# A state-space mixer on one NeuronCore: the gate of each group is projected two groups ahead instead of one

## What is computed

```
z, xbc, dt = split(h @ w_in)
xs, bm, cm = split(silu(dwconv(xbc)))
...
cb = einsum('bign,bjgn->bijg', ci, bi)
y = einsum('bijg,bijgr,bjgrp->bigrp', cb, decay, xdt)
y = y + einsum('bign,bigr,bgrpn->bigrp', ci, exp(cum), s)
...
y = (y_f + y_b[:, ::-1] + xs * d_gr)
return rms_norm_2(y * silu(z), norm_g) @ w_out
```

## Time and profile before

| | |
|---|---|
| Three runs | 2572.54, 2579.03, 2581.88 us; median 2579.03 us |
| The profiled execution | 2571.71 us, span 2570.1 us |
| PE busy | 2150.8 us, 84% of the span |
| DVE, ACT, POOL busy | 43%, 25%, 3% |
| Mean granted PE clock | 0.922 of full speed |
| The eight groups | from about 2152 us to 2296 us of the span |

### The profile page before, as it was taken

How to read it: one execution, slowest core, us unless ns; L and a number is a source line. 1 busy time by engine, 2 the same in 40 slices (tenths; PEclk the granted TensorE clock), 3 DMA queues, 4 the chain that set the end, 5 groups by cost and what they waited for, 6 DMA issues and landing times.

```text
span 2570.1 us, 31035 instructions
## 1 busy us (share of the span) xinstructions
PE 2150.8 (84%) x11646; PEld 1413.8 (55%) x11646; DVE 1110.2 (43%) x2058; ACT 644.6 (25%) x1212; POOL 68.8 (3%) x112
## 2 busy tenths in 40 slices
PE   6978688888968657885999878999977997997997
PEld 3457332334456422322445536888866886773996
DVE  0054321111153411112506535666673776863766
ACT  1134110111234100101302103111105544641332
POOL 1000100001000100001000000000010000000000
PEclk9979899999989788998999988999987997998999
DMA  6438779983448577985111021222211224323453
GB/s 190 140 111 276 255 305 401 406 328 122 140 148 284 177 295 310 406 329 196 66 66 66 33 82 66 99 99 99 99 55 59 100 73 154 118 92 138 174 187 115
DMA packets 153835, 440.42 MB, mean 171 GB/s; under 512 B 12176, under 2 KB 14656, under 8 KB 145360
## 3 DMA queue, kind: packets, MB, share of 16 engines
q1 hardware_dynamic: 145216, 414.88, 43.8%
q0 software_dynamic: 8464, 23.48, 3.0%
HBM read 534.63 MB, written 1.21 MB: 208 GB/s over the span
## 4 chain that ended last, share of the span: by engine, by line
PE 43%; ACT 4%; DVE 4%; DVEq 1%; issue 1%; DMA 1%; POOL 0%; ACTq 0%; SPq 0%; POOLq 0%
PE bank L1840 32%; PE bank L1914 10%; ACT UT L2208 1%; PE bank L1845 1%; DVE ARENA L2753 1%; ACT ARENA L2371 1%; DVE BN L2439 0%; ACT UH L2208 0%; DMA NEGM<-in_neg 0%; DVEq L2453 0%; DVE XA L2447 0%; ACT ARENA L2364 0%; ACT XHI L2208 0%; ACT ARENA L2184 0%; DMA ARENA<-cum_rows 0%
## 5 line engine op out<-in xcount | busy, mean ns | idle before, releaser
L604 PE MATMUL bank<-WA,XG 128*32 128x512 f32 x1536 | 187.5, 632 | 75.2 <-DMA WA<-in_expert_w_up 63.6
L1840 PE MATMUL bank<-W,UT 128*128 128x512 f32 (+2 forms) x704 | 238.2, 502 | 13.1 <-ACT XHI L2208 8.7
L464 PE MATMUL bank<-WD,XT 128*128 128x512 f32 (+1 forms) x576 | 239.9, 579 | 4.8 <-ACT XT L783 2.8
L2219 ACT ACTIVATE WPH<-W 128x1024 fp32r<-128x1024 f32 x128 | 135.4, 1070 | 371.3 <-PE bank L1840 198.2
L1840 PEld LDWEIGHTS bank<-W,UT 128*128 128x128 f32 x704 | 135.6, 204 | 114.2 <-issue 107.9
L1840 PE MATMUL bank<-UH,WPH 128*128 128x512 f32 (+1 forms) x512 | 174.0, 340 | 18.7 <-DVE WPL L2464 18.7
L464 PEld LDWEIGHTS bank<-WD,XT 128*128 128x128 f32 x576 | 109.7, 191 | 133.6 <-issue 128.4
L1840 PE MATMUL bank<-UL,WPH 128*128 128x512 f32 (+1 forms) x512 | 173.7, 339 | 0.0
L1840 PE MATMUL bank<-UH,WPL 128*128 128x512 f32 (+1 forms) x512 | 173.7, 339 | 0.0
L2464 DVE TENSOR_TENSOR WPL<-W,WPH 128x1024 fp32r<-128x1024 f32 x128 | 153.4, 1220 | 16.9 <-ACT WPH L2219 16.9
L604 PEld LDWEIGHTS bank<-WA,XG 128*32 128x32 f32 x1536 | 47.9, 115 | 204.0 <-issue 124.1
(11 more groups left out here) (370 smaller groups left out, 3345.7 us busy)
## 6 DMA issues: line engine op xcount, KB each, us to landing
WA<-in_expert_w_gate SPq DMA_DIRECT2D x32, 2048.0 KB
WA<-in_expert_w_up SPq DMA_DIRECT2D x32, 2048.0 KB
WC<-in_expert_w_down SPq DMA_DIRECT2D x32, 2048.0 KB
W<-in_ffn_w SPq DMA_DIRECT2D x64, 1024.0 KB, 6.6
WD<-in_ada_w SPq DMA_DIRECT2D x48, 1024.0 KB, 6.4
WA<-in_expert_w_gate SPq DMA_DIRECT2D x64, 512.0 KB
WA<-in_expert_w_up SPq DMA_DIRECT2D x64, 512.0 KB
WC<-in_expert_w_down SPq DMA_DIRECT2D x32, 1024.0 KB
```

Source lines behind the costliest of these rows:

```text
L464: last = nc.tensor.matmul(bank[r.bank(key)][:, 0:n], lhs[k], rhs[k], start=(k == 0), stop=(k == len(lhs) - 1))
L604: last = nc.tensor.matmul(bank[r.bank(key)][32 * g:32 * g + 32, :], xg[:, 4 * part + k, col:col + 32], WA[part][:, g, :, k, :], start=(par ...
L1840: return nc.tensor.matmul(bank[r.bank(key)][0:rows, cols[0]:cols[1]], lhs, rhs, start=start, stop=stop)
L2219: nc.scalar.activation(piece_view(WPH, q), piece_src(i, q), ACT.Copy).then_inc(hi_done, 1)
```

## The change

On PE `group_gate(1)` is issued behind `group_gate(0)`, ahead of the first group's outputs, and in turn g of the loop the gate of group g + 2 is projected instead of that of group g + 1. On ACT `gate(0)` is ahead of `segments(0)`, and `gate(g + 2)` stands in turn g where `gate(g + 1)` stood. Nothing else is changed: the banks, the two halves of Z and the lists of DVE, POOL and SP are the same.

```
             group_gate(0)
+            group_gate(1)
             for g in range(SG_):
                 group_outputs(g)
                 if g + 1 < SG_:
                     group_pre(g + 1)
-                    group_gate(g + 1)
+                if g + 2 < SG_:
+                    group_gate(g + 2)
                 if g >= 1:
                     group_turns(g - 1)
...
             act.wait_ge(x_whole, 1)
+            gate(0)
             segments(0)
             state_copy(0)
-            gate(0)
+            gate(1)
             act.wait_ge(ng_in, 16)
             for g in range(SG_):
                 if g + 1 < SG_:
                     segments(g + 1)
                     state_copy(g + 1)
-                    gate(g + 1)
+                if g + 2 < SG_:
+                    gate(g + 2)
                 if g >= 1:
                     turned_out(g - 1)
```

## The result

The changed kernel takes 2608.73 us (median of 4 runs, 2606.6 to 2615.26), the kernel before 2575.78 us (4 runs, 2572.49 to 2581.88). The ratio is 1.0129, with a 95% interval of 1.0099 to 1.0159: about 33 us slower. The profiled execution took 2615.26 us, span 2613.7 us.

A forecast was written before the change was run, and what follows sets the result against it. PE was taken to bound the loop before; the change's serial ACT-DVE chain adds 33.6 us up to T(7) and the end 3.9, so 37.5 us slower, 2616 from the median 2579.03; forecast 2615 us, range 2601 to 2624.

The forecast's parts named there:

- The start: Group 0: silu ahead of the exponentials, these 4.8 us late; PE's hole shrinks from 8.11 to about 5.1 us, clock low.
- T(0): End of group 0's 16 exponentials on ACT, put at 2173.36, 4.8 us late.
- The loop: Groups 2 to 7: waiting for `y_rdy` ahead of the exponentials makes a serial ACT-DVE chain, 21.8 us a turn against 16.4.
- six terms: Parts of a loop turn: 0.03, 1.37, 10.62 (DVE to `y_rdy`), 0.49, 0.85 and 8.42 us (load and exponentials), sum 21.8.
- the one term of 2.62 us: DVE's diagonals in each loop turn, counted within the 10.62 us of weights, diagonals and finish up to `y_rdy`.
- PE in time for the chain: In the loop PE's 15.66 us of work a turn fits the 21.8 us chain and costs it nothing, despite bank 2 waits.
- The end: Last outputs: PE idles some 9.6 us without a gate in turn 6, clock falls, `out_part` starts 3.9 us later relatively.
- T(7): End of group 7's 16 exponentials on ACT, put at 2317.8, 33.6 us later than before.
- The sum: Whole kernel: 33.6 + 3.9 = 37.5 us slower; 28.7 with the full clock throughout.
- The table load: ACT's function switches: 1.29 us from load to silu, no added drain; the skill page's 1.38 us would add about 8 us.
- The rival of the cold loop: PE runs the whole loop at the low clock, 31.3 us a turn, about 2663 us; chance 0.05.
- The rival of a gain: Hole at the start filled, `y_rdy` wait free, clock kept: up to 7.7 us faster, 2571 us; chance 0.02.

The follow-up runs named there:

- e1: The changed kernel with a third part of Z, so that gate(g) waits for the output of group g - 3; 2581.09 us, ratio to before 1.0031.
- e5: The changed kernel with DVE's finish of group g - 1 ahead of the diagonals of group g + 1; 2593.77 us, ratio to before 1.0084.
- e7: The changed kernel with the first half of each gate from group 2 on projected twice on PE; 2610.89 us in one execution.
- e2: The changed kernel with ACT's silus in the loop one group ahead as before, PE's order kept; 2613.44 us, ratio to before 1.0154.
- e4: The changed kernel with ACT's order of before, gates in two banks in turn and cb always in bank 1; 2566.30 us, ratio to before 0.9979.
- e9: e4 with half of the output projection's first quarter moved into turn 6 on PE; 2557.11 us, ratio to before 0.9939.
- e3: The kernel before with gate(0) moved ahead of segments(0) on ACT, nothing else; 2580.53 us in one execution.

## Why the prediction was right, point by point

The forecast was 2615 us in a range of 2601 to 2624, 37.5 us slower; it came out at 2608.73, 33 us slower by the medians and 35.7 us by the stage. That the profiled execution took 2615.26 us, almost the forecast, is luck: 8.5 us of it came from the first block.

- **The start.** The first exponentials were put 4.8 us late and the first outputs behind a hole of 5.1 us at the low clock. Measured from the stage's start, T(0) is 2181.94 - 2161.13 = 20.81 us against 15.96 before, 4.85 us late; the hole is 4.99 us, and the outputs take 11.23 us. Right. cb(1) came 11.3 us behind the outputs' start, for which I had 12.07.
- **The loop.** 21.8 us a turn were put together from six terms; it is 21.67 or 21.68 in each of the five turns. e1 removes the wait and the turns fall to 15.9 and 16.8 us; e5 removes the one term of 2.62 us and the turn falls to 19.1. Shown.
- **PE in time for the chain.** Right in that it costs nothing (e7), but the waits inside PE's turn were placed wrongly. I had the states wait 3.2 us for bank 2; what waits in the change is the wide outputs, for the banks that DVE's L2814 reads, and, as I had it, the small ones ahead of them, for `w_rdy`.
- **The end.** The step "there is no gate in turn 6, so PE idles some 9.6 us" held in its cost, not in its form. The turns wait 5.08 us for ACT's state_copy(7), which I hadn't seen, run slowly, and 1.18 us of hole follow. The projection starts 2340.12 - 2325.04 = 15.1 us behind T(7), for which I had 15.5.
- **The sum.** From the stage 37.5 was 1.8 us too much: 1.4 of it up to T(7), the rest at the end.
- **The table load.** The step from load to silu or exponential stayed at 2174.82 - 2173.53 = 1.29 us, and a turn is 21.68 us where the sum without a drain was 21.8. The drain that the Trainium skill, ScalarE: Activation LUTs, "What ACT_TABLE_LOAD costs", adds is not seen here. The one load less gave nothing: it would have stood in the 11.84 us in which ACT waits for PE.
- **The rival of the cold loop.** The clock did fall in each turn from group 2 on, for a part of it (0.77 in a window of 22 us), as the Trainium skill, TensorE: Matmul & The Clock Gate, "HAM oscillation", tells of waits in each iteration. It cost the loop nothing, because PE is off the chain there; in e2, where PE is on it, it did cost time.
- **The rival of a gain.** Its sum, up to 7.7 us faster, was for a kernel whose wait costs nothing. e1 is that kernel, and it is 8 us slower than before: this rival had left out the end, some 10 us, and its 5.6 us for a kept clock didn't come either, as e1's first outputs take 11.23 us like the change's. A gain needs the start without the first silu (e4) and the end covered (e9), 16 us in all.

## What to carry to other kernels

When work is moved ahead on an engine that works in order, list every wait that moves with it, and ask whether what it waits for needs something that now stands behind it; a buffer with two halves allows a distance of one, not of two. A shift by one turn fills a hole at the start and opens one at the end of the loop, so both ends are costed. To tell a chain from a busy engine, add work to the engine: the turn grows by that work only where the engine is the bound.

## What was not expected of the hardware

In e1 two equal holes of 0.99 us, two turns apart, were followed once by wide outputs of 2.82 us for x8 at a granted clock of 1.00, and once by the same outputs in 4.48 us, in a window whose mean clock was 0.67:

```profile
2238.22 2.82 PE L1840 MATMUL bank<-ARENA 128*128 128x512 f32 x8 [0.99 <-DVE YI L2814]
...
2270.92 4.48 PE L1840 MATMUL bank<-ARENA 128*128 128x512 f32 x8 [0.99 <-DVE YI L2814]
```

```profile
2236.00:2241.00 5.00, 4.01 (x21) 2.84 (x20) 4.52 (x13) 4.99 (x16) 0.00 (x0) 1.00 0.00 0
...
2271.00:2276.00 5.00, 5.00 (x10) 2.53 (x11) 3.61 (x11) 5.00 (x19) 0.00 (x0) 0.67 0.02 3
```

The kernel before has two such holes of 0.99 us with 2.82 us behind each, and e3 has one with 2.82 and one with 4.49 us. So behind a hole of 1 us PE lost half its clock for a few us, or lost nothing. What decides between the two was not settled here.
